# A hybrid decoder trunk: all four second halves of the last MLP as seven block products, and a changed order of VectorE's work around them

## The chip, the cores and the metric

The kernel runs on one core of one Trainium2 chip. The metric is the device time of one execution in microseconds. Timed executions of the kernel before took 1475.32, 1475.59 and 1476.76 us; the median, 1475.59 us, is the time before.

## The reference, cut to what matters

The program is two consecutive layers over 512 tokens of width 1024, in float32. Layer 0 has a recurrent mixer (RG-LRU and RWKV-7), layer 1 a retention mixer; after each mixer comes an MLP. Only the MLPs matter here:

```
def sq_relu_mlp(x, w_in, w_out):              # w_in 1024 x 4096, w_out 4096 x 1024
    return jnp.square(jax.nn.relu(x @ w_in)) @ w_out
...
f = sq_relu_mlp(rms_norm(h, norm_ffn_pre[layer]), ffn_w_in[layer], ffn_w_out[layer])
h = h + rms_norm(f, norm_ffn_post[layer])     # after the last layer, h is the output
```

## The kernel before, in words

**Products in three parts.** Every float32 operand of a large matmul is split into a high part of reduced precision (`...H`) and the rest (`...L`): ScalarE writes the high part (a copy with a change of type, `split_hi`, L336; activations L845), VectorE subtracts it from the whole for the low part (`split_lo`, L342). A product is then three matmuls: high x high, high x low, low x high. All the matmuls named here have 512 columns and contract over 128 rows.

**The weight stream.** All weights lie in memory as chunks of 128 x 2048 numbers (1 MB), in the order of their use. SyncE loads them one after the other into a ring of three places (L1941). It issues the load of chunk c when TensorE has started chunk c-2, which the semaphore `chunk_left` tells. Then ScalarE writes the chunk's high part and VectorE its low part, which stands over the raw weights; TensorE waits for `w_lo`. Each engine has its program written out by hand in a fixed order, so whatever stands first is done first, and an engine that waits holds up all that follows on it.

**An MLP** (`ffn_pe`, `ffn_act`, `ffn_dve`, L791 to L900) goes in four quarters of the 4096 hidden units. A quarter's first half has eight units j = 0 to 7, each one 128-row tile of hidden units for all 512 tokens: 24 matmuls into bank j % 4. VectorE applies the relu and the norm's factor (L873), squares (L881), ScalarE writes the high part `AH`, VectorE the low part `AL` (L884). Every two units use up one chunk, and after each even unit the chunk two ahead is split. The second half multiplies the squares with `w_out` and adds the result to `f` or `fT`.

**The last MLP's second halves.** In quarters 0, 1 and 2 (`q < SEVEN`, with `SEVEN = 3`) a second half is a product of two 2 x 2 block matrices, done with seven block products of half size in place of eight (the Strassen-Winograd scheme). The tokens are two halves of 256, the outputs two halves of 512, and the hidden units of the quarter two halves of 512. For it four sums and differences of activation blocks (`activation_sums`, L740, four VectorE operations on 128 x 256 after each of the units 4 to 7, split by `sums_high` and `sums_low`, L706 and L710) and four of weight blocks are needed. The weight sums are made during the first MLP: GpSimd loads a piece of the four blocks (1 MB), VectorE makes four operations on it (L780 to L786), GpSimd stores it to `sums_of_blocks` (L756 to L775); twelve pieces, four in each of the first MLP's quarters 0 to 2, after the odd units 9 to 15. Each of the seven products (`seven_pe`, L677) takes a chunk of its own, chunks c+4 to c+10, and two banks, one for each 128-token tile t of the half: 24 matmuls. `SEVEN_BANKS` (L673) are (4,5), (6,7), (0,1), (2,3), (4,5), (2,3), (4,5); the last three products are added in the banks to what an earlier one left there. VectorE's program (`seven_dve`, L720) has for each product i first the split of chunk c+6+i, then `sums_low` of the last sums (i = 1), and then the evacuation of the two banks of product i into `fT`.

**Quarter 3 and the end.** Quarter 3's second half is an ordinary product (`out_by_token_pe`, L573): for each half n of the outputs and each 128-token tile t, 24 matmuls of 512 columns into a bank of its own, 192 in all, from four chunks. After a bank is full, VectorE adds it to `fT` (L634) and multiplies by the gain row (L639), ScalarE squares and sums (L606). When a tile has both output halves, VectorE adds the two sums (L643), ScalarE takes the root (L610), VectorE the reciprocal (L650) and then the last operation on each half, `h + term * factor` (L624), after which SyncE stores it (L1946). The final operations of tile t-1 come between the gain term and the reciprocal of tile t. The gain row is loaded by GpSimd once `sums_lo` says that quarter 2's sums are done (L1973). In quarter 1's units 0 to 3 TensorE also transposes h into token order (`turn_h_pe`, L561, banks 4 to 7).

```
for i, banks in enumerate(SEVEN_BANKS):                                    # seven_dve, L720
    split_halves_lo(dve, c + 6 + i, 7 * q + i)
    if i == 1: sums_low(dve, q, 3)
    for t, b in enumerate(banks):
        dve.wait_ge(S(f"acc_full{b}"), u)
        ...                                                                # fT +/- bank[b]
```

## Time and profile before

| What | us |
|---|---|
| median of the timed executions | 1475.59 |
| the profiled execution, its own time | 1476.38 |
| its span in the trace | 1474.6 |
| TensorE busy in the span | 1434.8 |
| VectorE busy | 921.6 |
| ScalarE busy | 538.2 |
| GpSimd busy | 87.1 |

The trace is one execution, and its span is what the trace covers; 1.8 us of the execution's time lie around it. All times in the trace are microseconds from the span's start. An engine's busy time says how much it did, not whether anybody waited for it: TensorE's matmuls overlap, so its busy time is no measure of how near it is to its peak, and a wait of VectorE costs nothing unless TensorE or the last store stands behind it. The mean granted clock of TensorE was 0.986 of its full speed.

### The profile page before, as it was taken

Reading aid. Unit: us, or ns where it says so; the run is one execution under the profiler, and the core shown is the slowest. Engines: PE = TensorE matmul, PEld = TensorE weight load, DVE = VectorE, ACT = ScalarE, POOL = GpSimd, SP = SyncE. Lnnn points to the kernel's source line nnn. Section 1 sums busy time; section 2 is a strip of 40 time slices with the busy share of each in tenths; the row PEclk is TensorE's granted clock in tenths of the full one; section 3 lists DMA queues with packets and bytes.
Section 4 is the critical chain, followed back from the end, with each engine's and each line's share of the span. In section 5 each row is a group of like instructions: output and inputs, shape, how many; then the busy total and the mean of one; then the engine's idle time right before and its main releaser. Section 6 shows DMA issues by size and latency. Waiting matters only on the chain.

```text
span 1474.6 us, 22076 instructions
## 1 busy us (share of the span) xinstructions
PE 1434.8 (97%) x9650; PEld 1181.9 (80%) x9650; DVE 921.6 (63%) x1200; ACT 538.2 (36%) x632; POOL 87.1 (6%) x89
## 2 busy tenths in 40 slices
PE   9999999998999999998999999999998999999997
PEld 6778787777888888887888888888887788888786
DVE  7768676667655565654756445355447876868754
ACT  7555454533312222223343332332434433433322
POOL 0000000012010100001200000000003000000000
PEclk9999999998999999999999999999998999999999
DMA  5211111101474654731222122222130352434332
GB/s 187 73 36 59 50 59 45 59 30 42 178 266 143 224 181 175 263 112 60 86 68 100 62 86 92 81 86 86 62 110 29 132 182 86 171 115 166 134 110 62
DMA packets 30623, 160.21 MB, mean 109 GB/s; under 512 B 2816, under 2 KB 6912, under 8 KB 15552
## 3 DMA queue, kind: packets, MB, share of 16 engines
q1 hardware_dynamic: 23456, 130.73, 25.0%
q0 software_dynamic: 7072, 28.08, 5.4%
q8 instruction: 76, 1.25, 0.3%
q14 instruction: 19, 0.16, 0.0%
HBM read 144.12 MB, written 14.68 MB: 108 GB/s over the span
## 4 chain that ended last, share of the span: by engine, by line
PE 89%; DVE 6%; ACT 2%; issue 1%; DMA 1%; POOL 0%; DVEq 0%; POOLq 0%
PE bank L388 21%; PE bank L394 20%; PE bank L391 20%; PE bank L691 2%; PE bank L695 2%; PE bank L694 2%; PE bank L1681 2%; PE bank L1675 2%; PE bank L1678 2%; PE bank L993 2%; PE bank L402 1%; DMA raw<-weights 1%; PE bank L1000 1%; DVE WL L346 1%; PE bank L593 1%
## 5 line engine op out<-in xcount | busy, mean ns | idle before, releaser
L388 PE MATMUL bank<-XH,WH 128*128 128x512 f32 x944 | 379.4, 402 | 15.4 <-DVE XL L481 12.6
L391 PE MATMUL bank<-XL,WH 128*128 128x512 f32 x944 | 371.2, 393 | 0.0
L394 PE MATMUL bank<-XH,WL 128*128 128x512 f32 x944 | 371.0, 393 | 0.0
L346 DVE TENSOR_TENSOR WL<-raw,WH 128x2048 fp32r<-128x2048 f32 (+1 forms) x99 | 222.1, 2245 | 136.7 <-ACT WH L340 136.6
L340 ACT ACTIVATE WH<-raw 128x2048 fp32r<-128x2048 f32 (+1 forms) x99 | 185.2, 1872 | 189.9 <-DMA raw<-weights 189.8
L388 PEld LDWEIGHTS bank<-XH,WH 128*128 128x128 f32 x944 | 179.5, 190 | 58.8 <-issue 19.5
L394 PEld LDWEIGHTS bank<-XH,WL 128*128 128x128 f32 x944 | 179.4, 190 | 38.7
L391 PEld LDWEIGHTS bank<-XL,WH 128*128 128x128 f32 x944 | 179.7, 190 | 38.2 <-issue 2.1
L845 ACT ACTIVATE AH<-relu 128x512 fp32r<-128x512 f32 (+1 forms) x64 | 37.9, 592 | 216.4 <-DVE relu L873 216.4
L388 PE MATMUL bank<-AH,WH 128*128 128x512 f32 x256 | 99.7, 390 | 0.0
L391 PE MATMUL bank<-AL,WH 128*128 128x512 f32 x256 | 99.6, 389 | 0.0
L394 PE MATMUL bank<-AH,WL 128*128 128x512 f32 x256 | 99.6, 389 | 0.0
L552 DVE TENSOR_TENSOR f<-f,bank 128x512 f32<-128x512 f32 x64 | 43.0, 684 | 67.2 <-PE bank L394 67.0
L873 DVE SCALAR_TENSOR_TENSOR relu<-bank,rB 128x512 f32<-128x512 f32 x64 | 44.0, 688 | 64.9 <-PE bank L394 64.8
L388 PEld LDWEIGHTS bank<-AH,WH 128*128 128x128 f32 x256 | 48.0, 188 | 10.2 <-DVE AL L884 0.3
L394 PEld LDWEIGHTS bank<-AH,WL 128*128 128x128 f32 x256 | 48.0, 188 | 10.0
L391 PEld LDWEIGHTS bank<-AL,WH 128*128 128x128 f32 x256 | 48.0, 188 | 10.0
L388 PE MATMUL bank<-BH,WH 128*128 128x512 f32 x128 | 50.2, 392 | 0.3 <-DVE f L552 0.2
L394 PE MATMUL bank<-BH,WL 128*128 128x512 f32 x128 | 49.8, 389 | 0.0
L391 PE MATMUL bank<-BL,WH 128*128 128x512 f32 x128 | 49.8, 389 | 0.0
L1675 PE MATMUL bank<-WH,XH 128*128 128x512 f32 x128 | 49.8, 389 | 0.0
L1678 PE MATMUL bank<-WL,XH 128*128 128x512 f32 x128 | 49.8, 389 | 0.0
(360 smaller groups left out, 2339.3 us busy)
## 6 DMA issues: line engine op xcount, KB each, us to landing
raw<-weights SPq DMA_DIRECT2D x104, 1024.0 KB, 4.8
block<-weights POOLq DMA_DIRECT2D x12, 1024.0 KB, 7.6
sums_of_blocks<-block POOLq DMA_DIRECT2D x12, 1024.0 KB, 5.3
raw<-sums_of_blocks SPq DMA_DIRECT2D x12, 1024.0 KB, 4.8
raw<-weights SPq DMA_DIRECT2D x8, 512.0 KB, 4.5
h<-x_fm SPq DMA_DIRECT2D x4, 512.0 KB, 8.1
out_tm<-h SPq DMA_DIRECT2D x8, 256.0 KB, 2.6
rc<-ret_const POOLq DMA_DIRECT2D x1, 1536.0 KB, 8.1
```

What stands on the lines that cost most here:

```text
L340: nc.scalar.activation(WH[i][:, :n], raw[i][:, :n], ACT.Copy).then_inc(S("w_hi"), 1)
L346: nc.vector.tensor_tensor(WL[i][:, :n], raw[i][:, :n], WH[i][:, :n], ALU.subtract).then_inc(S("w_lo"), 1)
L388: mm = pe.matmul(bank[b][:], wh, xh, start=(k == 0), stop=False)
L391: mm = pe.matmul(bank[b][:], wh, xl, start=False, stop=False)
L394: mm = pe.matmul(bank[b][:], wl, xh, start=False, stop=(k == len(xs) - 1))
L552: nc.vector.tensor_tensor(f[:, m, :], f[:, m, :], bank[b][:], ALU.add).then_inc(S(f"acc_free{b}"), 1)
L691: mm = pe.matmul(bank[b][:], xh, wh, start=(k == 0 and not ADDED[i]), stop=False, skip_group_check=True)
L694: pe.matmul(bank[b][:], xh, wl, start=False, stop=False, skip_group_check=True)
L845: nc.scalar.activation(AH[:, j, :n], relu[:, j % 2, :n], ACT.Square).then_inc(S("a_hi"), 1)
L873: nc.vector.scalar_tensor_tensor(relu[:, j % 2, :], bank[b][:], 0.0, rB[:], ALU.max, ALU.mult).then_inc(S(f"acc_free{b}"), 1)
L1675: mm = pe.matmul(bank[2 + t][:], XH[:, kt, tok], wh, start=(kt == 0), stop=False)
L1678: mm = pe.matmul(bank[2 + t][:], XH[:, kt, tok], wl, start=False, stop=False)
```

## The change

`SEVEN` goes from 3 to 4 (`QUARTERS`): quarter 3's second half of the last MLP is also done with seven block products, and `out_by_token_pe`, `out_by_token_act` and `out_by_token_dve` are gone. Its norm and stores go by token half: token tiles 0 and 1 are complete with product 5, tiles 2 and 3 with product 6, which closes both output halves of a tile at once. The weight stream gets three more chunks (11 in the quarter instead of 8), and the first MLP four more pieces of weight sums, in its quarter 3 after the odd units 1 to 7. The gain terms are kept where X was. In `seven_dve` the evacuation of product i stands ahead of the split of chunk c+6+i. In the last MLP's first halves the split of chunk c+5, at unit 6, stands ahead of `sums_low` and `activation_sums` of that unit. ScalarE's order in the first halves is not changed.

```diff
@@ -46,9 +46,9 @@
 FFN1_CHUNK = RET_CHUNK0 + 8 * RET_HEADS
 
 
-SEVEN = 3
+SEVEN = QUARTERS
 FFN1_AT = [FFN1_CHUNK + 11 * q for q in range(SEVEN + 1)]
-ALL_CHUNKS = FFN1_AT[SEVEN] + 8
+ALL_CHUNKS = FFN1_AT[SEVEN]
...
-        uT = nc.alloc_sbuf_tensor_at("uT", [P, TT, D], F32, offset=start)
+        uT = nc.alloc_sbuf_tensor_at("uT", [P, TT, D], F32, offset=x_at)
...
 
@@ -698,10 +615,63 @@
         def seven_act(act, use, c, q):
             for i, banks in enumerate(SEVEN_BANKS):
                 split_halves_hi(act, c + 6 + i, 7 * q + i)
-                for b in banks:
-                    use.next(b)
+                now = [use.next(b) for b in banks]
                 if i == 0:
                     sums_high(act, q, 3)
+                if q < QUARTERS - 1:
+                    continue
+                for t, b in enumerate(banks):
+                    if i in (1, 5):
+                        act.wait_ge(S(f"acc_free{b}"), now[t])
+                        out_square(act, t, i // 5)
+                    if i == 6:
+                        act.wait_ge(S("first_final"), t + 1)
+                        out_square(act, 2 + t, 0)
+                        act.wait_ge(S(f"acc_free{b}"), now[t])
+                        out_square(act, 2 + t, 1)
+                        out_root(act, 2 + t)
+                if i == 5:
+                    out_root(act, 0)
+                    out_root(act, 1)
+
+
+
+        OUT_ORDER = [(0, 0), (1, 0), (0, 1), (1, 1), (2, 0), (2, 1), (3, 0), (3, 1)]
+
+        def out_part(x, t, n):
+            return x[:, t, n * T:(n + 1) * T]
+
+        def out_square(act, t, n):
+            k = OUT_ORDER.index((t, n))
+            if k >= 2:
+                act.wait_ge(S("token_squares"), k - 1)
+            nc.scalar.activation(hn[:, k % 2, :], out_part(fT, t, n), ACT.Square,
+                                 accum_out=squares[:, n, t:t + 1]).then_inc(S("token_squares"), 1)
+
+        def out_root(act, t):
+            act.wait_ge(S("token_sum"), t + 1)
+            nc.scalar.activation(post_root[:, t:t + 1], squares[:, 2, t:t + 1], ACT.Sqrt, bias=epsc[:, 0:1],
+                                 scale=1.0 / D).then_inc(S("token_root"), 1)
+
+        def out_term(dve, t, n):
+            dve.wait_ge(S("gain_loaded"), 16)
+            nc.vector.tensor_tensor(out_part(uT, t, n), out_part(fT, t, n), gain_row[:, n * T:(n + 1) * T],
+                                    ALU.mult).then_inc(S("token_term"), 1)
+
+        def out_sum(dve, t):
+            dve.wait_ge(S("token_squares"), OUT_ORDER.index((t, 1)) + 1)
+            nc.vector.tensor_tensor(squares[:, 2, t:t + 1], squares[:, 0, t:t + 1], squares[:, 1, t:t + 1],
+                                    ALU.add).then_inc(S("token_sum"), 1)
+
+        def out_stored(dve, t):
+            dve.wait_ge(S("token_root"), t + 1)
+            nc.vector.reciprocal(post_rstd[:, t:t + 1], post_root[:, t:t + 1]).then_inc(S("token_rstd"), 1)
+            dve.wait_ge(S("token_rstd"), t + 1)
+            dve.wait_ge(S("h_by_token"), 2 * TT)
+            for n in range(2):
+                dve.wait_ge(S("token_term"), OUT_ORDER.index((t, n)) + 1)
+                u, at = out_part(uT, t, n).rearrange("p (k c) -> p k c", c=P), hT[t][:, 4 * n:4 * n + 4, :]
+                nc.vector.scalar_tensor_tensor(at, u, post_rstd[:, t:t + 1], at, ALU.mult, ALU.add).then_inc(S("out_ready"), 1)
...
@@ -719,9 +689,6 @@
 
         def seven_dve(dve, use, c, q):
             for i, banks in enumerate(SEVEN_BANKS):
-                split_halves_lo(dve, c + 6 + i, 7 * q + i)
-                if i == 1:
-                    sums_low(dve, q, 3)
                 for t, b in enumerate(banks):
                     u = use.next(b)
                     dve.wait_ge(S(f"acc_full{b}"), u)
@@ -735,7 +702,28 @@
                             ins = nc.vector.tensor_scalar(to, bank[b][:], float(sign), None, ALU.mult)
                         else:
                             ins = nc.vector.tensor_tensor(to, to, bank[b][:], ALU.add if sign > 0 else ALU.subtract)
+                        if q == QUARTERS - 1 and i == 6 and outputs == 0:
+                            ins.then_inc(S("first_final"), 1)
                     ins.then_inc(S(f"acc_free{b}"), 1)
+                    if q == QUARTERS - 1 and i in (3, 5):
+                        last = added[0, i // 5, t]
+                        dve.wait_ge(S(f"acc_free{last[0]}"), last[1])
+                        out_term(dve, t, i // 5)
+                    if q == QUARTERS - 1 and i == 6:
+                        dve.wait_ge(S("first_final"), t + 1)
+                        out_term(dve, 2 + t, 0)
+                        dve.wait_ge(S(f"acc_free{b}"), u)
+                        out_term(dve, 2 + t, 1)
+                        out_sum(dve, 2 + t)
+                split_halves_lo(dve, c + 6 + i, 7 * q + i)
+                if i == 1:
+                    sums_low(dve, q, 3)
+                if q == QUARTERS - 1 and i >= 5:
+                    for t in range(2):
+                        if i == 5:
+                            out_sum(dve, t)
+                    for t in range(2):
+                        out_stored(dve, 2 * (i - 5) + t)
...
@@ -767,7 +755,7 @@
 
 
 
-                pool.wait_ge(S("a_lo"), 8 * (n // 4) + 4 + n % 4)
+                pool.wait_ge(S("a_lo"), min(8 * (n // 4) + 4 + n % 4, 24))
                 load(n)
...
-                        if layer and q < SEVEN and j > 4:
+                        if layer and j == 6:
+                            split_lo(dve, c + 5)
+                        if layer and j > 4:
                             sums_low(dve, q, j - 5)
-                        if layer and q < SEVEN and j >= 4:
+                        if layer and j >= 4:
                             activation_sums(dve, q, j - 4)
                     else:
                         add_to_f(dve, use, b, j - 8, q == 0)
                         if q == QUARTERS - 1 and j in (12, 14):
                             post_sum_dve(dve, m, j // 2 - 6)
-                    if j % 2 == 0 and (q or j):
+                    if j % 2 == 0 and (q or j) and not (layer and j == 6):
                         split_lo(dve, c + j // 2 + 2)
-                    if not layer and q < SEVEN and j in (9, 11, 13, 15):
-                        weight_sums_dve(dve, 4 * q + j // 2 - 4)
-                if layer and q < SEVEN:
+                    if not layer and j in ((1, 3, 5, 7) if q == QUARTERS - 1 else (9, 11, 13, 15)):
+                        weight_sums_dve(dve, 4 * q + j // 2 % 4)
+                if layer:
                     seven_dve(dve, use, c, q)
-                elif layer:
-                    out_by_token_dve(dve, use, c, q)
 
```

The rest of the diff takes the three `out_by_token` functions away with their calls, makes `chunk_source` take the sums in all four quarters, lets the two halves of a split return where the stream is at its end, and takes `q < SEVEN` out of the conditions.

## Rows read from the trace of the kernel before

**Rows 1.** The page, part 1: busy us (share of the span) xinstructions.
```profile
PE 1434.8 (97%) x9650; PEld 1181.9 (80%) x9650; DVE 921.6 (63%) x1200; ACT 538.2 (36%) x632; POOL 87.1 (6%) x89
```

**Rows 2.** Table by stretches (start:end, length, busy us of PE, PEld, DVE, ACT, POOL, clock, DMA).
```profile
1168.48:1210.42 41.94, 40.05 (x169) 32.52 (x168) 33.80 (x43) 18.19 (x19) 0.00 (x0) 0.96 0.50 175
1257.94:1296.02 38.08, 38.08 (x169) 31.53 (x168) 28.98 (x34) 14.50 (x15) 0.00 (x0) 1.00 0.54 194
1339.54:1379.08 39.54, 38.33 (x169) 31.46 (x168) 28.89 (x34) 14.75 (x16) 0.58 (x1) 1.00 0.56 199
...
1422.60:1466.12 43.52, 43.52 (x193) 35.86 (x191) 18.93 (x29) 10.31 (x20) 0.00 (x0) 1.00 0.18 61
```

**Rows 3.** The list of waits, last MLP, TensorE: in total, times, longest.
```profile
PE bank L691 <- DVE WL L346: 1.9, 1, 1.9
PE bank L691 <- DVE fT L737: 1.2, 1, 1.2
PE bank L563 <- DVE fT L737: 0.2, 1, 0.2
```

**Rows 4.** Timeline of VectorE in quarter 2: start us, us, engine, line, operation.
```profile
1336.43 1.22 DVE L712 TENSOR_TENSOR S_low<-S_both,S_high 128x1024 fp32r<-128x1024 f32 x1
...
1339.22 2.28 DVE L346 TENSOR_TENSOR WL<-raw,WH 128x2048 fp32r<-128x2048 f32 x1
1341.42 0.68 DVE L873 SCALAR_TENSOR_TENSOR relu<-bank,rB 128x512 f32<-128x512 f32 x1
...
1347.41 1.22 DVE L361 TENSOR_TENSOR WL<-raw,WH 128x1024 fp32r<-128x1024 f32 x1
...
1367.28 1.28 DVE L737 TENSOR_TENSOR fT<-fT,bank 128x512 f32<-128x512 f32 x2
1368.48 1.22 DVE L359 TENSOR_TENSOR WL<-raw,WH 128x1024 fp32r<-128x1024 f32 x1
```

**Rows 5.** Timeline of ScalarE in quarter 2.
```profile
1335.62 1.90 ACT L340 ACTIVATE WH<-raw 128x2048 fp32r<-128x2048 f32 x1
1339.33 1.06 ACT L708 ACTIVATE S_high<-S_both 128x1024 fp32r<-128x1024 f32 x1 [1.81 <-DVE S_both L752]
```

**Rows 6.** Timeline of TensorE in quarter 0, starts of products 1 and 2.
```profile
1175.97 0.50 PE L691 MATMUL bank<-WH,AH 128*128 128x512 f32 x1 [1.89 <-DVE WL L346]
...
1183.20 0.40 PE L691 MATMUL bank<-WH,AH 128*128 128x512 f32 x1
```

**Rows 7.** Timeline of ScalarE and VectorE in quarter 0.
```profile
1170.03 1.91 ACT L340 ACTIVATE WH<-raw 128x2048 fp32r<-128x2048 f32 x1
...
1175.83 0.68 DVE L873 SCALAR_TENSOR_TENSOR relu<-bank,rB 128x512 f32<-128x512 f32 x1
...
1181.82 1.22 DVE L361 TENSOR_TENSOR WL<-raw,WH 128x1024 fp32r<-128x1024 f32 x1
```

**Rows 8.** Landing of ring loads (first), GpSimd's gain row, landing of blocks of weights.
```profile
DMA to landing us min/median/max: 4.7/4.8/7.6
...
1355.12 0.58 POOL L1973 DMA_DIRECT2D gain_row<-last_gain  x1 [219.22 <-DVE S_low L712]
...
DMA to landing us min/median/max: 4.6/5.8/8.5
```

**Rows 9.** Timeline of VectorE, the end.
```profile
1460.88 0.69 DVE L634 TENSOR_TENSOR fT<-fT,bank 128x512 f32<-128x512 f32 x1 [0.49 <-PE bank L593]
1461.67 0.69 DVE L639 TENSOR_TENSOR uT<-fT,gain_row 128x512 f32<-128x512 f32 x1
...
1468.33 1.42 DVE L624 SCALAR_TENSOR_TENSOR h<-uT,small,h 128x512 f32<-128x512 f32 x2
...
1469.86 1.42 DVE L624 SCALAR_TENSOR_TENSOR h<-uT,small,h 128x512 f32<-128x512 f32 x2
```

**Rows 10.** Table by stretches, after the two long waits.
```profile
1177.20:1180.65 3.45, 3.45 (x9) 2.63 (x9) 3.27 (x7) 1.88 (x2) 0.00 (x0) 0.51 0.90 302
1368.40:1384.00 15.60, 15.60 (x70) 12.92 (x69) 11.26 (x15) 4.08 (x5) 0.00 (x0) 1.00 0.60 203
```

## What I predict, and why

> **What bounds the kernel now.** I read the page first, for the busy shares: TensorE is busy for 97% of the span [rows 1]. Then the table by stretches, for the last MLP. Its second halves have 168 matmuls in seven-product form and take 38.08 us when nothing disturbs them; the last quarter's ordinary half has 192 and takes 43.52 us [rows 2]. Both are one matmul per 0.2267 us, so a matmul removed is worth 0.2267 us as long as TensorE never waits. Quarter 0's seven products take 41.94 us and quarter 2's 39.54, so there something did wait. Third, the list of waits says what: once the low halves of a weight chunk (1.9 us), once an `fT` evacuation (1.2), once a bank that the transposes of h want (0.2) [rows 3]. Last, the timelines of VectorE and ScalarE around those waits. TensorE bounds everything but these places and the last 8 us.
>
> I number the products 0 to 6 (they use chunks c+4 to c+10), write R for the start of product 0, and call "chain" VectorE's row of work from unit 6 of the first half to the low half of chunk c+6, which product 2 needs.
>
> **Part 1, fewer matmuls.** Quarter 3 goes from 192 to 168: 43.52 - 38.08 = **-5.44 us** [rows 2].
>
> **Part 2, the split of chunk c+5 ahead of the sums.** In quarter 2 VectorE ends `AL` of unit 6 and is free at about 1336.43. The split now comes here, but it waits for ScalarE's high half, which ends at 1335.62 + 1.90 = 1337.52 [rows 4, 5]. Nothing stands before it any more to fill that time: VectorE idles 1.1 us, and all behind it (sums, unit 7, split of c+6) is 1.1 later, as the split is only exchanged with the sums (2.20 us from its start to the next operation). Also, the sums of unit 6 now end just before unit 7's relu, so ScalarE makes `S_high` (1.06 us [rows 5]) ahead of unit 7's `AH`, and `AL` waits about 0.3 more.
>
> **Part 3, banks read ahead of splits.** The chain gets product 0's two evacuations in front of the split of c+6: 1.20 us from the start of a pair to the next operation on VectorE (1367.28 to 1368.48 [rows 4]). So the low half of c+6, done at 1347.41 + 1.22 = 1348.63 before, comes at 1348.63 + 1.13 + 0.28 + 1.20 = 1351.24. Product 2 would start at R + 2 x 5.44 = 1339.54 + 10.88 = 1350.42. It waits **0.86 us**. Before, the chain had 1.8 us to spare. Quarter 1 has the same spacing (38.08 us, no wait), and quarter 3 becomes a copy of it: **3 x 0.86 = +2.6 us**. Bounds: 0, since with the evacuations alone (1349.83) it would be in time, and 4.1, with another half microsecond of dispatch in each chain. I take the sum of the rows.
>
> **Quarter 0** has no slack, since its first half starts late behind the norm. Before, product 1 waited for its chunk until 1175.97, and product 2 began at 1183.20 [rows 6], just as VectorE had finished c+6 (1181.82 + 1.22 = 1183.04 [rows 7]). After: c+5's high half ends at 1170.03 + 1.91 = 1171.94 [rows 7], its low half at 1174.27, so product 1 starts 1.65 us earlier. But its fourth weight tile needs `AL` of unit 7, and unit 7's relu moves from 1175.83 to 1177.0: `AL` is ready at 1179.4. TensorE does nine matmuls to 1176.4 and waits 3.0 us: the wait is changed, not removed. c+6 comes at 1183.04 + 1.16 + 0.28 + 1.19 = 1185.67, and product 2 at 1185.72: **+2.5 us**, whatever product 1 does before. Bounds 1.2 (only the evacuations ahead) and 4.1 (with a clock fall inside product 2, below).
>
> **Waits that go.** The transposes find their banks free: **-0.2** [rows 3]. Quarter 2's wait is double. Chunk c+9 landed in 7.6 us instead of the median 4.8 [rows 8], beside the gain row, which GpSimd issued at 1355.12 [rows 8]; and product 3's evacuations stood behind the split of it, which freed bank 2 only at 1368. The gain row now waits for quarter 3's sums, so quarter 2 loses the whole 39.54 - 38.08: **-1.5**. Quarter 3 inherits the collision, the issues being as close as before (1.2 us); only the evacuation is no longer behind it, and that is the time from the split's end (1367.3 [rows 4]) to TensorE's restart (an evacuation of 0.68 and the handover): 1.5 - 0.8 = **+0.7** (0 to 1.5).
>
> **The end.** Write X for the end of product 5. Its second bank is read at X + 0.20; 0.79 later its gain term starts (1460.88 to 1461.67 [rows 9]), 0.69 later the sum of squares; ScalarE's root and the reciprocal put the first final operation at X + 2.5. Token tiles 0 and 1 take two each; two such pairs take 2.95 us (1468.33 to 1469.86 + 1.42 [rows 9]): VectorE is busy to X + 5.4. Bank 4 of product 6 is full at X + 2.9 but is read only then, since the stores of tiles 0 and 1 stand before it. Tile 2 needs two evacuations (1.2), two gain terms (1.3) and a sum: X + 7.9. Tile 3 the same: X + 10.4. Then both tiles' reciprocals and four final operations, 0.2 and again 2.95 us: X + 13.6. TensorE's last result is at X + 5.44 + 0.16 (a matmul is shown 0.39 long, and the next starts after 0.23), so VectorE ends 8.0 us after it, against 1471.28 - (1466.12 + 0.16) = 5.0 before: **+3.0 us**. What is new is that product 6 closes two output blocks of a tile at once (two evacuations, two terms), and that tiles 0 and 1 are in the way. The last four stores are spaced as before, so nothing for them. Bounds: +0.8, if tile 2's evacuations and terms found room before bank 5 is full (X + 5.6 + 2.6 + 3.2 = X + 11.4), and +4.
>
> **The first MLP.** Four more pieces of weight sums in its quarter 3, 4 x 4 x 0.69 = 11 us of VectorE and 8 MB of transfers. Per two units (10.88 us) VectorE there does 2 x 2.1 (relu, square, low) + 2.2 (split) + 2.8 = 9.2, so it keeps up. A block lands in 4.6 to 8.5 us [rows 8], issued about 8 us before it is wanted; a late one delays `AL`, with 1.3 us in hand for unit 7 in the worst line-up. I take 0; up to +1.5 if two land late. The table for the rotary angles goes out 50 us later, still some 50 ahead of its use.
>
> **Sum.** -5.4 + 2.6 + 2.5 - 0.2 - 1.5 + 0.7 + 3.0 = +1.7 us. The profiled execution took 1476.38 us (span 1474.6 and 1.8 around it), 0.8 above the median 1475.59. So 1478.1 against it, **1477.3** against the median: the removed matmuls pay for a longer end and for a VectorE chain that is now late at product 2.
>
> **Rivals.**
> *Slower, by the clock.* After the 2.05 us gap in quarter 0 the granted clock was 0.51 of 2.4 GHz, the 1.2 GHz level, for 3.45 us, with 9 matmuls where 15 would go [rows 10]: 6 x 0.23 = 1.4 us. Quarter 0 now has two gaps in a row, 3.0 us in product 1 and 1.2 before product 2. A fall after the first is inside the time that VectorE sets, but a fall that comes late, into product 2, adds 1.4: 1478.7. It decides from the point where product 2 starts at half clock. If the 0.9 us waits of quarters 1 to 3 also do it, 3 x 1.4 more: 1482.9. Against that: after the 1.4 us wait of quarter 2 the clock stayed 1.00 [rows 10]. The Trainium skill ("TensorE: Matmul & The Clock Gate", section "Why this matters for your kernels") only warns of idle gaps longer than that one; the trace disagrees, so the measurement decides, and by the page waits of 0.9 and 1.2 us cost no clock and the time stays 1477.3.
> *Faster, the chain is on time.* If product 2 does not wait in quarters 1 to 3 (2.6) and quarter 0 is as before (2.5): 1472.2. For it: only 0.9 us is missing. Against: four dependent rows, each from the trace.
> *The first MLP's VectorE falls behind*, +1.5 or more: 1478.8 and up. For it: landings grew along quarter 2, up to 8.5 us.
> *The end costs little*: with a VectorE end of 5 us as before, 1474.3; against it, 2.95 us of final operations stand before tile 2.
>
> **How the numbers follow.** About 0.2% (3 us) is what can be told from no change. My forecast with its own range 1474.5 to 1478.5 gets 0.56; a cheap end 0.05, still within; faster by the chain 0.13; late clock fall 0.14, all waits cost the clock 0.03, first MLP behind 0.09. The late fall and the first MLP lie at the bound of 1478.5, so nearly all of them count as slower: 0.25. Faster 0.13, same 0.62. The range 1473.5 to 1480.5 leaves out most of the last rival and part of the fast one.
>
> **What would show it.** Right: seven products of quarter 0 about 44.5 us, of quarters 1 and 2 about 38.9, of quarter 3 about 39.7; a TensorE wait on `WL` of about 0.9 us before product 2; a VectorE wait of 1 us on ScalarE before the split of c+5; VectorE ending 8 us after TensorE. Wrong: quarters 1 and 2 at 38.1, or an end of 5 us; a gap in the first MLP would mean a cost I set at nothing.

## The result, and the profile after

The changed kernel took 1487.09 us (median of 4 executions, 1485.27 to 1488.55) against 1475.85 (4 executions, 1475.32 to 1476.76) of the kernel before: a ratio of 1.007 with the 95% interval [1.0054, 1.0086]. I had said 1477.3. The forecast was 10 us too low, and outside its range.

The page of the changed kernel, part 1 (busy us, share of the span, instructions), answers to [rows 1]: 24 matmuls fewer, VectorE 32 us busier.

```profile
span 1485.8 us, 22125 instructions
PE 1436.7 (97%) x9626; PEld 1181.6 (80%) x9626; DVE 953.7 (64%) x1252; ACT 546.9 (37%) x644; POOL 93.1 (6%) x97
```

The last MLP by stretches, the seven products of quarters 0 to 3, in the columns of [rows 2]:

```profile
1178.30:1222.88 44.58, 40.58 (x169) 32.43 (x168) 35.15 (x45) 18.05 (x19) 0.00 (x0) 0.96 0.45 165
1270.14:1309.35 39.21, 38.42 (x170) 31.46 (x169) 31.19 (x41) 14.98 (x16) 0.00 (x0) 1.00 0.52 188
1352.81:1391.99 39.18, 38.39 (x170) 31.45 (x169) 31.24 (x41) 14.83 (x16) 0.00 (x0) 1.00 0.54 188
1435.50:1474.81 39.31, 38.52 (x169) 31.19 (x167) 33.83 (x50) 15.85 (x23) 0.58 (x1) 1.00 0.44 158
```

TensorE's waits in the last MLP, as in [rows 3] (waits in total, how many, the longest):

```profile
PE bank L608 <- DVE WL L365: 3.3, 4, 1.0
PE bank L608 <- DVE AL L867: 2.9, 1, 2.9
PE bank L608 <- DVE WL L346: 0.2, 1, 0.2
```

These are the waits I had worked out: four on the low half of a chunk before product 2, at most 1.0 us (I said 0.9 and 1.2), and 2.9 in quarter 0's product 1 for `AL` of unit 7 (I said 3.0). So the last MLP went nearly as forecast, and most of the loss lies elsewhere. The two traces, laid beside each other matmul by matmul, give it. The table cuts the span at the 5901st matmul (in the first MLP's quarter 3, before its second half) and at the first matmul of product 0 of the last MLP. In both kernels the same matmuls run up to the second cut.

| stretch | before, us | after, us | difference |
|---|---|---|---|
| to matmul 5901 | 634.39 | 638.07 | +3.7 |
| to product 0 of the last MLP | 534.09 | 540.25 | +6.2 |
| to the end of the span | 306.08 | 307.50 | +1.4 |
| span | 1474.56 | 1485.82 | +11.3 |

**The middle stretch** holds a gap that the kernel before doesn't have. TensorE in the changed kernel, at the start of the first MLP's second half of quarter 3 (start, duration, line, operation, idle time before it and what ended it):

```profile
656.66 0.39 PE L398 MATMUL bank<-AH,WL 128*128 128x512 f32 x1
660.48 0.50 PE L392 MATMUL bank<-AH,WH 128*128 128x512 f32 x1 [3.44 <-DVE AL L867]
660.82 0.54 PE L395 MATMUL bank<-AL,WH 128*128 128x512 f32 x1
661.16 0.63 PE L398 MATMUL bank<-AH,WL 128*128 128x512 f32 x1
```

It waits 3.44 us for `AL` of unit 7, and its matmuls are then longer: from 660.9 to 664.3 the granted clock is 0.50 of 2.4 GHz, the 1.2 GHz level. The wait and the slow clock together are 5.3 of the 6.2 us. VectorE shows why `AL` is late:

```profile
645.46 0.69 DVE L867 TENSOR_TENSOR AL<-squared,AH 128x512 fp32r<-128x512 f32 x1
650.10 0.69 DVE L768 TENSOR_TENSOR block<-block 128x512 f32<-128x512 f32 x1 [3.95 <-DMA block<-weights]
...
652.88 0.68 DVE L856 SCALAR_TENSOR_TENSOR relu<-bank,rB 128x512 f32<-128x512 f32 x1
...
656.08 2.29 DVE L346 TENSOR_TENSOR WL<-raw,WH 128x2048 fp32r<-128x2048 f32 x1 [1.04 <-ACT WH L340]
658.28 0.68 DVE L856 SCALAR_TENSOR_TENSOR relu<-bank,rB 128x512 f32<-128x512 f32 x1
...
659.74 0.69 DVE L867 TENSOR_TENSOR AL<-squared,AH 128x512 fp32r<-128x512 f32 x1
```

VectorE was free at 646.15, behind `AL` of unit 5, and stood 3.95 us before a block of weights that had not landed. Unit 6's relu, the split and unit 7's relu are in the same row behind it. `AL` of unit 7 was done at 660.43; TensorE wanted it at 657.05. By these rows it would have been in time without that wait, which experiment 3 tests. GpSimd's own timeline shows when the block had been asked for:

```profile
638.98 0.76 POOL L761 DMA_DIRECT2D sums_of_blocks<-block  x1 [10.15 <-DVE block L774]
639.73 0.75 POOL L752 DMA_DIRECT2D block<-weights  x1
653.44 0.77 POOL L761 DMA_DIRECT2D sums_of_blocks<-block  x1 [12.96 <-DVE block L774]
654.20 0.75 POOL L752 DMA_DIRECT2D block<-weights  x1
```

A block is asked for only behind the store of the piece before it, which waits for that piece's sums. This one went out at 639.73, 6.4 us before VectorE was free for it, and took 10.3. Over the whole execution, who waits for blocks, and how long the loads alone take to land (least, median, most); first the kernel before, then the changed one:

```profile
DVE block L780: 15.0, 9
DMA to landing us min/median/max: 5.4/7.6/8.5
```

```profile
DVE block L768: 26.1, 13
DMA to landing us min/median/max: 5.3/7.7/10.3
```

The last line of [rows 8], 4.6/5.8/8.5, which the prediction goes by, is not of the loads alone: it mixes the 12 loads of blocks with the 12 stores of their sums, which land in 4.6 to 6.2. The page of the kernel before gives the loads' median too:

```profile
block<-weights POOLq DMA_DIRECT2D x12, 1024.0 KB, 7.6
```

So the kernel before already showed the lateness: VectorE waited 15 us for blocks, nine times. The nine are the loads that go out right behind a store. They were asked for 5.2 to 7.1 us before VectorE was free for them and took 7.5 to 8.5, so every one came late; the other three, one at the head of each quarter, were asked for 21 us and more ahead. No wait of TensorE lies in that stretch, because the pieces all stood behind units 9, 11, 13 and 15, in second halves, where VectorE only adds to `f`. The new four stand behind units 1, 3, 5 and 7. They were asked for 6.2 to 6.4 us ahead, took 7.8, 7.7, 10.3 and 9.2, and VectorE waited 1.4, 1.3, 4.0 and 3.0 us for them; only the third, behind unit 5, reached TensorE.

**The first stretch** cannot come from the change in this way: both kernels issue the same work there. The difference is the clock. A table by stretches (columns as [rows 2]) of the changed kernel, and the same stretch in the kernel before:

```profile
83.70:95.60 11.90, 11.61 (x114) 8.55 (x110) 4.25 (x7) 3.94 (x6) 0.00 (x0) 0.57 0.01 3
```

```profile
83.70:95.60 11.90, 10.88 (x126) 8.52 (x127) 5.76 (x9) 7.73 (x11) 0.00 (x0) 1.00 0.00 1
```

Granted clock 0.57 against 1.00. Whether that comes with the changed kernel or only with this execution of it is a question for the runs.

### The profile page after: what moved, and what is told of

The parts are those of the page before. It is cut to its first block, busy times and chain, and to the rows that moved or that the text cites. A ratio compares the mean times of both kernels' runs of the same rounds, so it can differ in the third digit from the quotient of the medians.

```text
span 1485.8 us, 22125 instructions
## 1 busy us (share of the span) xinstructions
PE 1436.7 (97%) x9626; PEld 1181.6 (80%) x9626; DVE 953.7 (64%) x1252; ACT 546.9 (37%) x644; POOL 93.1 (6%) x97
## 4 chain that ended last, share of the span: by engine, by line
PE 76%; DVE 11%; issue 8%; ACT 3%; POOL 2%; DMA 1%; DVEq 0%; POOLq 0%
PE bank L392 17%; PE bank L398 16%; PE bank L395 16%; PE bank L608 2%; PE bank L611 2%; PE bank L612 2%; PE bank L1661 2%; PE bank L1658 2%; PE bank L1664 2%; PE bank L976 2%; DVE WL L346 2%; PE bank L406 2%; PE bank L983 1%; ACT WH L340 1%; DVE S_low L682 1%
## 5 line engine op out<-in xcount | busy, mean ns | idle before, releaser
L346 DVE TENSOR_TENSOR WL<-raw,WH 128x2048 fp32r<-128x2048 f32 (+1 forms) x97 | 217.6, 2245 | 130.0 <-ACT WH L340 130.0
L340 ACT ACTIVATE WH<-raw 128x2048 fp32r<-128x2048 f32 (+1 forms) x97 | 181.4, 1872 | 184.4 <-DMA raw<-weights 184.4
L398 PEld LDWEIGHTS bank<-AH,WL 128*128 128x128 f32 x256 | 48.4, 189 | 10.2
L355 ACT ACTIVATE WH<-raw 128x1024 fp32r<-128x1024 f32 x26 | 27.6, 1060 | 71.7 <-DMA raw<-weights 36.4
L704 DVE TENSOR_TENSOR fT<-fT,bank 128x512 f32<-128x512 f32 x56 | 36.9, 682 | 20.8 <-PE bank L612 20.8
L608 PE MATMUL bank<-WH,S_high 128*128 128x512 f32 x128 | 49.9, 390 | 0.0
```

Source lines behind the costliest of these rows:

```text
L340: nc.scalar.activation(WH[i][:, :n], raw[i][:, :n], ACT.Copy).then_inc(S("w_hi"), 1)
L346: nc.vector.tensor_tensor(WL[i][:, :n], raw[i][:, :n], WH[i][:, :n], ALU.subtract).then_inc(S("w_lo"), 1)
L398: mm = pe.matmul(bank[b][:], wl, xh, start=False, stop=(k == len(xs) - 1))
L608: mm = pe.matmul(bank[b][:], xh, wh, start=(k == 0 and not ADDED[i]), stop=False, skip_group_check=True)
L704: ins = nc.vector.tensor_tensor(to, to, bank[b][:], ALU.add if sign > 0 else ALU.subtract)
```

## The experiments

Theory: the four further pieces of weight sums make the middle stretch longer, because a late block holds VectorE where `AL` hangs on it. Rivals: the new orders in the last MLP cost more than the trace shows; or the whole kernel runs at a lower clock. Each ratio below is to executions of the kernel before on the same chip.

**1. The pieces alone, and everything but the pieces.** sums_only is the kernel before with the four further pieces (and with the count of `AL` tiles that a load waits for held at 24, as in the change); nothing reads them.

```diff
-            pieces = [(q, ...) for q in range(SEVEN) for j in range(PIECES)]
+            pieces = [(q, ...) for q in range(QUARTERS) for j in range(PIECES)]
-                    if not layer and q < SEVEN and j in (9, 11, 13, 15):
-                        weight_sums_dve(dve, 4 * q + j // 2 - 4)
+                    if not layer and j in ((1, 3, 5, 7) if q == QUARTERS - 1 else (9, 11, 13, 15)):
+                        weight_sums_dve(dve, 4 * q + j // 2 % 4)
```

> The kernel before, with only the four further pieces of weight sums in the first MLP's quarter 3 (loaded, summed and stored as in the changed kernel; nothing reads them). Theory P, the blocks land late: TensorE waits for AL of unit 7 in the first MLP by 3 to 4 us and the clock falls behind it, together +5.2 us, 1481 us. Theory E, the rest of the loss in front of the last MLP (3.8 us at 84 us into the span, where the granted clock is at half for 10 us although neither the program nor the data differ there) belongs to how the program lies in time or in memory, not to the sums: then it is absent or present here regardless of the pieces. If it is present: 1485. Rival R, the pieces cost nothing and all of the loss comes from elsewhere: 1476.

no_new_sums is the changed kernel without them. Its quarter 3 multiplies with quarter 2's sums, so that part of the output is not what the reference computes.

```diff
-                    return sums_of_blocks[q, k]
+                    return sums_of_blocks[min(q, SEVEN - 2), k]
-            pieces = [(q, ...) for q in range(SEVEN) for j in range(PIECES)]
+            pieces = [(q, ...) for q in range(SEVEN - 1) for j in range(PIECES)]
```

> The changed kernel without the four further pieces; quarter 3 reads the sums of quarter 2 in their place (that part of the result is left out). Theory P: the first MLP is as before, so 5.2 us less than the changed kernel, 1482, and if the early half clock goes as well, 1477 to 1478, which is what was predicted for the last MLP alone. Rival R (the pieces cost nothing): 1487.

Measured: sums_only 1484.91 us (ratio 1.0037 [1.0025, 1.005] to the kernel before, 12 executions against 30), in the mean 5.5 us more. no_new_sums 1481.31 (1.0019 [1.0006, 1.0032]), in the mean 2.6 more. sums_only's middle stretch is 7.3 longer than before, no_new_sums' is 534.07, as before; their last stretches are 306.21 and 307.80. The two parts stand in different places and add up, to 8.1 us.

**2. The last MLP's two orders, each taken back.**

```diff
@@ split_back: the split of chunk c+5 is behind the sums again
-                        if layer and j == 6:
-                            split_lo(dve, c + 5)
-                    if j % 2 == 0 and (q or j) and not (layer and j == 6):
+                    if j % 2 == 0 and (q or j):
@@ evac_back: in seven_dve the split is ahead of the evacuations again
+                split_halves_lo(dve, c + 6 + i, 7 * q + i)
+                if i == 1:
+                    sums_low(dve, q, 3)
```

> The changed kernel with the split of chunk c+5 back behind the sums of unit 6. Theory C (the chain): VectorE no longer idles 1.1 us, the waits before product 2 in quarters 1 to 3 go (0.95 us each), quarter 0's seven products take about 1.2 us less: 4 us less than the changed kernel, 1483. Rival S (the split ahead of the sums is what keeps TensorE from waiting longer before product 1): quarter 0 gets its 2 us wait back and nothing is won, 1487.

> The changed kernel with the split of chunk c+6+i back in front of the evacuation of product i. Theory C: product 0's two evacuations no longer stand before the split of c+6 (1.2 us), so the wait before product 2 goes in quarters 1 to 3 (0.95 each) and quarter 0 loses 1.2 less; against it product 5 of quarter 3 waits again for the evacuation behind the late chunk (1.4): net 2.5 less, 1484.5. Rival B (banks read late hold TensorE up more than once): 1488 or more.

Measured: split_back 1484.25 us (1.0033 [1.0019, 1.0047]), its seven products 43.10, 38.08, 38.08 and 38.11 us, its last stretch 302.57. evac_back 1484.98 (1.0043 [1.0027, 1.0058]), products 43.63, 38.08, 38.08 and 38.08, last stretch 303.71. Either order taken back removes the waits of quarters 1 to 3 completely; the last stretch gets 4.9 and 3.8 us shorter. So the wait before product 2 in these quarters is the sum of two delays of one chain, each of which alone is absorbed. In quarter 0, which has no slack, neither is free: 43.10 and 43.63 us against 41.94 before. The 1.4 us that evac_back was expected to lose at product 5 of quarter 3 did not appear (38.08). TensorE's waits in split_back:

```profile
PE bank L608 <- DVE WL L346: 1.8, 1, 1.8
PE bank L608 <- DVE WL L365: 0.9, 1, 0.9
```

The 2.9 us for `AL` in quarter 0 is gone, and 1.8 for the low half of c+5 is back, as before the change.

**3. Is it the landing?** prefetch is the changed kernel with each block asked for one piece earlier, ahead of the store of the piece before it. The two buffers get a counter of stores each.

```diff
-                pool.wait_ge(S("a_lo"), min(8 * (n // 4) + 4 + n % 4, 24))
-                load(n)
+                while loaded <= n or loaded == n + 1 < len(pieces) and (loaded % 4 or loaded >= 12):
+                    pool.wait_ge(S("a_lo"), min(8 * (loaded // 4) + 4 + loaded % 4, 24))
+                    load(loaded)
+                    loaded += 1
```

> The changed kernel with the blocks for the weight sums loaded one piece ahead: the load of piece n+1 is issued before the wait for the sums of piece n, where it stood behind the store of piece n. Theory P (the landing is what is late): VectorE no longer waits for blocks in the first MLP's quarter 3, TensorE has no wait for AL of unit 7, the first MLP takes 72.8 us where the changed kernel takes 76.6 to 77.3, 4 to 5 us less in all. Rival V (VectorE simply has too much work there: 9.2 us in each 10.9): the wait for AL shrinks but stays over 1 us. Rival D (two loads and a store together slow each other): the landings grow beyond 10 us and nothing is won.

Measured: 1479.49 us, 1.0005 [0.999, 1.002]. The middle stretch is 534.08, to a hundredth that of the kernel before. The loads of blocks take nearly as long to land:

```profile
DMA to landing us min/median/max: 5.5/7.5/9.1
```

but they are now asked for 11 us or more ahead and none is waited for, with the same four pieces of sums on VectorE. Here are `AL` of units 6 and 7 and the start of the piece behind unit 7:

```profile
645.38 0.69 DVE L868 TENSOR_TENSOR AL<-squared,AH 128x512 fp32r<-128x512 f32 x1
...
650.82 0.69 DVE L868 TENSOR_TENSOR AL<-squared,AH 128x512 fp32r<-128x512 f32 x1
651.43 0.68 DVE L769 TENSOR_TENSOR block<-block 128x512 f32<-128x512 f32 x1
```

So neither the 11 us of VectorE nor the 8 MB is what costs, but the place at which a block is asked for. The landing times belong beside the Trainium skill ("DMA: Bandwidth & Descriptors", section "Anatomy of one DMA — SWDGE (gpsimd) path"), which gives 2.0 us and the bytes at 436 GB/s, an estimate of 4.4 us for 1 MB. The traces disagree, and the measurements decide: the fastest load of a block took 5.3 us, the median one 7.7, and the slowest in the changed kernel's first profile 10.3, beside the stores and the ring's loads.

**4. A better version.** orders is prefetch with the split of c+5 behind the sums again, and the split of c+6 alone ahead of product 0's evacuations; the later evacuations stay ahead of the splits.

```diff
+                if i == 0:
+                    split_halves_lo(dve, c + 6, 7 * q)
...
-                split_halves_lo(dve, c + 6 + i, 7 * q + i)
+                if i:
+                    split_halves_lo(dve, c + 6 + i, 7 * q + i)
```

> The changed kernel with blocks one piece ahead, the split of chunk c+5 back behind the sums of unit 6, and the split of c+6 ahead of product 0's evacuation, while all later products are still evacuated ahead of splits. Theory C: the seven products take 38.1 us in quarters 1 to 3 and 41.9 in quarter 0 as before; from product 0 of quarter 0 to the end 301.4 (before: 306.1, changed: 307.5), and the first MLP as before: 4.7 us less than the kernel before. Rival (product 1 of quarter 0 holds it up): 302.6, as with the split alone put back.

best moves, beside that, the four gain terms of token tiles 2 and 3 from VectorE to GpSimd.

> As the run orders, and the four gain terms of token tiles 2 and 3 made by GpSimd instead of VectorE. Theory W (the end is VectorE's work, 13.4 us of it in a row from product 5's end): four operations of 0.65 less make the end 1.6 us shorter at least, as GpSimd's four take 1.3 each beside it: 299.8 from product 0 to the end. Rival G (GpSimd's operations slow VectorE's, or are themselves last): no gain, 301.4 or more.

seven_only is prefetch with all of VectorE's old orders: the fourth quarter in seven-product form and nothing else.

> As the run orders, with VectorE's old order everywhere in the last MLP: the split of c+5 behind the sums, every split c+6+i ahead of the evacuation of product i. So it is the kernel before with quarter 3 in seven products, blocks one piece ahead. Theory C: from product 0 of quarter 0 to the end 302 to 303.7, as quarter 3 may wait 1.5 us for the evacuation behind the late chunk; the median within 2 us of the run orders, about 1475. Rival B (reading banks ahead of splits is worth more than that one wait): over 304 us, and 1477 or more.

| kernel | median us | ratio to before [95%] | seven products of quarters 0 to 3 | last stretch |
|---|---|---|---|---|
| prefetch | 1479.49 | 1.0005 [0.999, 1.002] | 44.69 / 39.19 / 39.15 / 39.56 | 307.79 |
| orders | 1474.50 | 0.9965 [0.9948, 0.9981] | 42.02 / 38.08 / 38.08 / 38.79 | 302.18 |
| best | 1478.29 | 0.999 [0.9971, 1.0009] | 42.17 / 38.08 / 38.08 / 38.08 | 303.11 |
| seven_only | 1477.37 | 0.9984 [0.9967, 1.0001] | 42.02 / 38.08 / 38.08 / 38.81 | 303.38 |

orders beats both kernels: 0.35% under the kernel before. orders and seven_only have the same products within 0.02 us and last stretches 1.2 us apart; the rest of the 2.9 between their medians I can't place, and their intervals overlap. In both, product 5 of quarter 3 starts late behind a chunk that landed in 7.5 and 6.9 us beside the gain row's load (4.8 in the median, [rows 8]), which costs 0.7 us; in the changed kernel's profile next to nothing of this shows (39.31 against 39.2).

best's profile doesn't have that 0.7, but split_back and evac_back don't either, with the terms on VectorE, so it isn't shown that the edit wins it. best loses at the end: from the last matmul to the end of the span 12.75 us against 11.26, which makes its last stretch 0.9 longer than that of orders. The rest of the 3.8 between their medians stays open. VectorE in best, between GpSimd's terms, and in orders; first the two lines of best:

```profile
1460.33 1.26 DVE L663 TENSOR_TENSOR squares<-squares 128x1 f32<-128x1 f32 x1 [0.80 <-ACT hn L648]
1463.59 1.18 DVE L663 TENSOR_TENSOR squares<-squares 128x1 f32<-128x1 f32 x1 [0.81 <-ACT hn L648]
```

GpSimd in best:

```profile
1459.08 2.48 POOL L698 TENSOR_TENSOR uT<-fT,gain_row 128x512 f32<-128x512 f32 x2 [22.41 <-DVE fT L717]
1462.26 2.49 POOL L698 TENSOR_TENSOR uT<-fT,gain_row 128x512 f32<-128x512 f32 x2 [0.70 <-DVE fT L717]
```

and the line L663 of orders, where GpSimd is idle:

```profile
L663 DVE TENSOR_TENSOR squares<-squares x4: 149/152/159, 1459.5 to 1467.9; 128x1 f32<-128x1 f32 x4
```

A sum of one element per partition takes 0.15 us alone, and 1.26 and 1.18 us where it starts while GpSimd multiplies; each ends just when GpSimd's pair does (1461.56 and 1464.75). The Trainium skill ("GPSIMD Engine Reference", section "8. Key points") says that GpSimd shares its SBUF interfaces with VectorE, with contention for VectorE's operations with two SBUF inputs; the trace agrees, and by its numbers the small operation, seen twice, lasts until the large ones are done.

**5. The early half clock.** changed_again is the changed kernel, unaltered; before_look1, before_look2 and before_look3 are one execution each of the kernel before.

> The changed kernel, unaltered, for its time beside the others and beside more executions of the kernel before. Theory L (where the clock happens to fall in the first mixer and the norms is chance, for either kernel): the executions of both scatter by some 8 us, the difference of the medians is what the two MLPs account for, 5.2 + 1.4 = 6 to 7 us, and the half clock at 84 us is there in some executions of either. Rival M (the changed program always draws the half clock at 84 us and the kernel before never): the difference stays at 11 us.

> The kernel before, unaltered, for another profile of it. Theory L (chance): in some executions of the kernel before the granted clock is at half at 84 to 95 us, and matmul 1200 then starts 4 to 5 us later. Rival M: never.

> The same as before_look1, one more profile: theory L has the half clock at 84 us in about half of such looks, rival M in none.

> The same as before_look1, one more profile: theory L has the half clock at 84 us in about half of such looks, rival M in none.

changed_again took 1488.49 us (1.0066 [1.0043, 1.0089]), in the mean 9.9 us more than the kernel before, which is nearer the rival's 11 than the 6 to 7 of the theory of chance. It again had half clock at 85.4 us, for 10.2 us, and once more at 37.6. The three executions of the kernel before (1476.86, 1476.48, 1475.62 us) had neither, where the theory of chance wanted about half. By then sums_only, split_back, evac_back and changed_again had the stretch near 85 us, and no_new_sums, prefetch, orders and best had not: it looked as if it came with the late blocks, 300 us ahead of the first of them. seven_only spoke against that: it has no late blocks, and its stretch is

```profile
83.70:95.60 11.90, 11.45 (x148) 8.58 (x148) 3.90 (x7) 2.72 (x4) 0.00 (x0) 0.57 0.01 3
```

Three further runs were made to settle it: the changed kernel twice more, and no_new_sums once more (again with quarter 2's sums in quarter 3).

> The changed kernel, unaltered. Half-clock stretches near 38 and 85 us stand in its two profiles and in none of the five of the kernel before, though both programs are the same there; seven_only, whose first MLP keeps the early blocks, has them too. Theory A (they come and go from execution to execution, whatever the kernel): the mean granted clock over these executions is 0.982 to 0.983 against the kernel before's 0.984 (the changed kernel's own stretch of 3.4 us at 661 us lowers it by 0.0012), the mean excess over the kernel before is 8 us or less, and at least one profile of the changed kernel has no half clock at 84 us. Theory B (the changed kernel has them for a reason): mean clock 0.981 or less again, excess 9.5 us or more, and all profiles with the half clock at 84 us.

> As changed_more1: theory A mean granted clock 0.982 to 0.983 and a profile without the half clock at 84 us in at least one of the two; theory B mean clock 0.981 or less and the half clock at 84 us in both.

> The changed kernel without the four further pieces of weight sums in the first MLP, and its quarter 3 reads the sums of quarter 2 (that part of the output is left out). Theory A: 1.5 to 3 us over the kernel before in the mean (the first took 2.6: 1.7 of the last MLP and the rest scatter). Theory B (the last MLP's edits lower the clock ahead of themselves): 3 us or more, with mean clock 0.982 or less against 0.984.

changed_more1, the same program as changed_again, has in that stretch

```profile
83.70:95.60 11.90, 10.82 (x132) 8.40 (x128) 5.76 (x9) 7.32 (x10) 0.00 (x0) 1.00 0.01 3
```

and no_new_more, which has no late blocks, has 0.57 there. The early half clock comes and goes between executions of one program, the changed one. For the kernel before this isn't shown: none of its four profiles has it near 85 us, against 7 of the 13 profiles of the other kernels. By stretches, in all profiles, as the difference to the first profile of the kernel before:

| kernel | to matmul 5901 | to product 0 | to the end | span |
|---|---|---|---|---|
| before_look1 / 2 / 3 | +0.4 / 0.0 / -0.9 | -0.1 / -0.1 / 0.0 | +0.2 / +0.2 / +0.2 | +0.5 / +0.1 / -0.7 |
| after | +3.7 | +6.2 | +1.4 | +11.3 |
| changed_again | +3.8 | +7.0 | +1.3 | +12.1 |
| changed_more1 | -0.2 | +4.3 | +1.7 | +5.8 |
| changed_more2 | +2.4 | +9.7 | +2.4 | +14.5 |
| sums_only | +2.9 | +7.3 | +0.1 | +10.3 |
| split_back | +4.6 | +6.2 | -3.5 | +7.4 |
| evac_back | +7.0 | +3.9 | -2.4 | +8.5 |
| no_new_sums | +1.6 | 0.0 | +1.7 | +3.3 |
| no_new_more | +3.7 | -0.3 | +2.1 | +5.5 |
| prefetch | +0.7 | 0.0 | +1.7 | +2.4 |
| seven_only | +6.9 | +0.9 | -2.7 | +5.1 |
| orders | +2.1 | +1.7 | -3.9 | -0.2 |
| best | -0.4 | -0.1 | -3.0 | -3.5 |

The first column follows no edit. The second is 3.9 to 9.7 in the seven profiles with late blocks that reach `AL`, and -0.3 to +1.7 in the others. changed_more1 took 1484.35 us (1.0032 [1.0019, 1.0046]), changed_more2 1489.05 (1.0056 [1.0036, 1.0077]), no_new_more 1479.96 (1.001 [0.9995, 1.0025]). In the mean changed_more1 and changed_more2 together are 6.8 us above the kernel before with a mean granted clock of 0.983 against 0.984: as the theory of chance had it, unlike changed_again. no_new_more was 1.3 us above, a little less than that theory's 1.5 to 3.

TensorE's waits for `AL` differ too between these executions: 3.2 us in changed_more1, 6.0 in two waits in changed_more2 (window from 630 to 705 us):

```profile
PE bank L392 <- DVE AL L867: 6.0, 2, 4.4
```

And the clock doesn't always fall behind such a wait. In changed_more1 TensorE's first matmul behind it, and the stretch that follows (columns as [rows 2]):

```profile
656.36 0.50 PE L392 MATMUL bank<-AH,WH 128*128 128x512 f32 x1 [3.16 <-DVE AL L867]
```

```profile
656.40:659.80 3.40, 3.40 (x15) 2.80 (x16) 0.00 (x0) 0.00 (x0) 0.00 (x0) 1.00 0.70 286
```

That is one reason why its middle stretch is only 4.3 us longer.

All executions together: 28 of the changed kernel have a mean of 1486.9 us, 103 of the kernel before 1478.9. The difference is 8.0 us, not the 11.2 of the first comparison, whose four executions of the kernel before lie at the low end of its 103.

## Why the prediction was wrong

**The step that failed** is the last of the sum: "The first MLP. [...] I take 0; up to +1.5 if two land late." It measured +5.5 us in the mean of 12 executions (sums_only; its profiled middle stretch was 7.3 longer), and prefetch, which only asks for the blocks earlier, gives it back: 1.0 us over the kernel before in the mean. That it is a cost of this kind was named ("a late one delays `AL`"); its size was wrong for three reasons.

- The landing. "4.6 to 8.5 us [rows 8]" is read from a row that mixes loads and stores. The loads that go out behind a store took 7.5 to 8.5 us in the kernel before, all nine of them, and with four more pieces one took 10.3.
- The lead. I took a block to be asked for "about 8 us before it is wanted". No row showed that: the nine had 5.2 to 7.1 us, and the four new ones 6.2 to 6.4, since the store of the piece before stands ahead of the load in GpSimd's order and waits for that piece's sums. With such leads and landings a late block is the rule and not the exception, and the kernel before could have told it.
- The place. I counted VectorE's work against TensorE's (9.2 of 10.88 us) instead of asking where in the half VectorE's lateness is felt: the kernel before waited 15.0 us for blocks at places where it doesn't matter.

The rival ("+1.5 or more: 1478.8 and up", 0.09) was what happened; it had too small a chance and no upper end. In the first profile the clock's fall behind the wait, 3.4 us at half clock and so 1.7 us lost, is a part of the cost; in changed_more1 there is no fall.

**The last MLP** was right as a sum (+1.7 forecast; +1.4, +1.3, +1.7 and +2.4 in four profiles) and nearly in its terms:

| term | forecast | measured (first profile) |
|---|---|---|
| seven products of quarter 0, 41.94 before | 44.5 | 44.58 |
| of quarter 1 | 38.94 | 39.21 |
| of quarter 2 | 38.94 | 39.18 |
| quarter 3, second half, 43.52 before | 39.6 | 39.31 |
| the end: start of the last matmul to the end of the span, 8.67 before | +3.0 | 11.24, +2.6 |
| the transposes | -0.2 | no such wait |

Product 2 starts 0.95 us late, not 0.86 (and the written sum, 1351.24 less 1350.42, gives 0.82), and with the slower first matmuls behind the wait the seven products take 1.1 more than 38.08. VectorE waits 1.04 us on ScalarE before the split of c+5 (said: 1.1), and unit 7's `AL` 0.38 and 0.39 on `AH` in quarters 0 and 2 (said: 0.3). VectorE ends 7.6 us after TensorE (1482.53 against 1474.97; said: 8.0), in the order that I wrote down:

```profile
1473.13 1.42 DVE L674 SCALAR_TENSOR_TENSOR h<-uT,small,h 128x512 f32<-128x512 f32 x2
1474.46 1.28 DVE L704 TENSOR_TENSOR fT<-fT,bank 128x512 f32<-128x512 f32 x2
1475.66 1.29 DVE L658 TENSOR_TENSOR uT<-fT,gain_row 128x512 f32<-128x512 f32 x2
...
1481.12 1.41 DVE L674 SCALAR_TENSOR_TENSOR h<-uT,small,h 128x512 f32<-128x512 f32 x2
```

The one miss in it: quarter 3's inherited collision was to cost 0.7 and cost 0.1 (in changed_again nothing, in changed_more2 0.9, in orders 0.7). So that the last stretch came out at +1.4 for a forecast of +1.7 is in part luck: quarters 1 to 3 and the collision missed to opposite sides.

**The rivals.** The late fall of the clock in quarter 0 didn't happen: the half clock (3.4 us from 1190.0) fell into product 1, ahead of the wait that VectorE sets, and the quarter took what the waits alone give. Nor did the 0.9 us waits cost the clock: 1.00 in quarters 1 to 3. The chain on time happened only when one of the two orders was taken back, and was worth 3.8 to 4.9 us as against my 5.1; with both taken back (orders) it was 5.3.

**The rest of the miss** is the comparison itself. Of the first 11.2 us, 8.0 hold over many executions. 5.5 and 2.0 (the mean over no_new_sums and no_new_more) make 7.5 of them. The other 3.2 are of the size of the early half clock (+3.7 in the first stretch), which stood in the profile of the changed kernel and not in that of the kernel before. I had put what can be told from no change at 3 us; one comparison of four executions each is off by as much. What decides in which executions the clock falls at 38 and 85 us stays open: the two programs do the same there. So does whether it is quite as frequent in both: changed_again had a mean clock of 0.9806 in its 9 executions, changed_more1 and changed_more2 0.983 in 15, the kernel before 0.984 in 99, and a fall like that at 661 us, 3.4 us long, accounts for 0.001.

## What to carry over

Work that a second engine does in a shadow must be weighed by the place where its lateness lands, not by its sum: ask of every wait of the kernel before that cost nothing what stood behind it, and whether the new copy stands in front of something else. A load issued behind a store that waits for the result of the load before it makes one chain out of two buffers; asking one piece earlier took its cost away without touching an engine's work. And where two edits delay one chain with slack, price them together: in quarters 1 to 3 each alone was free, and both together cost 1.1 us a quarter. Last, see what a row of landing times covers: loads and stores under one name have a median that neither has.

## What the runs showed of the hardware

- The granted clock of one unaltered program differs between executions: at 83.7 to 95.6 us it was 0.57 in the first profile of the changed kernel and 1.00 in changed_more1, and the timed executions of the kernel before range from 1474.47 to 1485.05 us with mean clocks of 0.986 to 0.979.
- A wait of TensorE for `AL` at the same place was followed by a granted clock of 0.50 for 3.4 us when it was 3.44 us long (first profile) and by 1.00 when it was 3.16 us long (changed_more1).
- A 128x1 sum on VectorE took 1.26 us instead of 0.15 beside a 128x512 multiplication of GpSimd, until GpSimd's pair was done.
- GpSimd's 1 MB loads landed in 5.3 us at best. In the kernel before, the nine that went out right behind a 1 MB store took 7.5 to 8.5, the other three 5.4 to 6.9; in the changed kernel's first profile the slowest took 10.3.
